# Third mixer's attention by pairs of heads, and heads turned between the chunks of the first two output panels

## What is computed

```python
h = concat(meta, x)                                   # 272 x 1024
for i in range(2):
    h = h + 0.5 * rmsnorm(swiglu(rmsnorm(h)))         # feed-forward, width 2816
    hn = rmsnorm(h)
    m = neighborhood_attention(hn) if i == 0 else diff_attention(hn)
    h = h + rmsnorm(m)
    h = h + 0.5 * rmsnorm(swiglu(rmsnorm(h)))
x = h[16:]                                            # 256 tokens from here on
x = x + rms_norm(hybrid_mixer(rms_norm(x)))           # third mixer
x = x + rms_norm(mlp(rms_norm(x)))                    # width 4096
```

## Time and profile before

| | before |
|---|---|
| median of 3 runs | 1523.96 us (1520.89 to 1527.64) |
| profiled execution, its own time | 1518.83 us |
| its span in the trace | 1517.0 us, granted TensorE clock 0.99 |
| TensorE busy | 1460.0 us (96%) |
| VectorE busy | 955.2 us (63%) |
| ScalarE busy | 659.0 us (43%) |
| GpSimd busy | 53.2 us (4%) |

### The profile page before, as it was taken

One profiled execution on the slowest core, in us unless ns is written; L12 is line 12 of the kernel. 1 busy time (PEld: TensorE's weight loads), 2 busy tenths in 40 slices (PEclk: granted clock), 3 DMA queues, 4 the chain that ended last, 5 costly groups with the idle time before them and its releaser, 6 DMA issues.

```text
span 1517.0 us, 27189 instructions
## 1 busy us (share of the span) xinstructions
PE 1460.0 (96%) x11458; PEld 1404.6 (93%) x11458; DVE 955.2 (63%) x1229; ACT 659.0 (43%) x856; POOL 53.2 (4%) x75
## 2 busy tenths in 40 slices
PE   6999999999999999999999998999999998999998
PEld 5999999978999999999999977899999996999997
DVE  5665567457766646665547566766646657877644
ACT  4444345445544335434335345553434533444432
POOL 0000010011000000000010000100001010100000
PEclk9999999999999999999999999999999999999998
DMA  5555884512455665654464510465555640355551
GB/s 179 171 188 166 224 238 148 175 35 84 140 167 180 177 191 153 195 185 153 149 192 149 170 54 29 141 193 183 173 162 161 197 137 1 112 179 182 193 188 63
DMA packets 250779, 233.52 MB, mean 154 GB/s; under 512 B 29759, under 2 KB 249844, under 8 KB 250688
## 3 DMA queue, kind: packets, MB, share of 16 engines
q1 hardware_dynamic: 250224, 231.96, 49.4%
q10 hardware_dynamic: 464, 0.25, 0.1%
HBM read 230.99 MB, written 1.12 MB: 153 GB/s over the span
## 4 chain that ended last, share of the span: by engine, by line
PE 79%; DVE 10%; issue 4%; ACT 3%; DMA 2%; POOL 1%; SPq 0%; DVEq 0%; ACTq 0%
PE acc L582 23%; PE acc L583 23%; PE acc L584 23%; DVE h L1553 2%; PE aux L747 1%; DVE h L1547 1%; ACT w_hi L1125 1%; DVE rstd L1518 1%; DVE x_lo L1524 1%; PE acc L889 1%; PE acc L919 1%; PE aux L869 1%; PE aux L910 1%; DMA raw<-in_ffn_w_up 1%; DVE h L1608 1%
## 5 line engine op out<-in xcount | busy, mean ns | idle before, releaser
L582 PE MATMUL acc<-x_hi,w_hi 128*128 128x272 f32 (+1 forms) x2096 | 599.2, 286 | 10.5 <-DVE z L1639 6.2
L583 PE MATMUL acc<-x_lo,w_hi 128*128 128x272 f32 (+1 forms) x2096 | 599.9, 286 | 0.0
L584 PE MATMUL acc<-x_hi,w_lo 128*128 128x272 f32 (+1 forms) x2096 | 597.9, 285 | 0.0
L1513 DVE TENSOR_TENSOR w_lo<-raw,w_hi 128x2048 fp32r<-128x2048 f32 (+1 forms) x230 | 483.9, 2113 | 88.5 <-ACT w_hi L1125 88.0
L1125 ACT ACTIVATE w_hi<-raw 128x2048 fp32r<-128x2048 f32 (+3 forms) x251 | 406.6, 1627 | 138.2 <-DMA raw<-in_ffn_w_down 49.6
L582 PEld LDWEIGHTS acc<-x_hi,w_hi 128*128 128x128 f32 x2096 | 396.8, 189 | 12.6 <-issue 10.1
L583 PEld LDWEIGHTS acc<-x_lo,w_hi 128*128 128x128 f32 x2096 | 395.6, 189 | 0.1
L584 PEld LDWEIGHTS acc<-x_hi,w_lo 128*128 128x128 f32 x2096 | 395.6, 189 | 0.0
L582 PE MATMUL acc<-hid_hi,w_hi 128*128 128x272 f32 (+1 forms) x704 | 204.5, 290 | 6.5 <-DVE w_lo L1513 6.5
L583 PE MATMUL acc<-hid_lo,w_hi 128*128 128x272 f32 (+1 forms) x704 | 203.0, 288 | 0.0
L584 PE MATMUL acc<-hid_hi,w_lo 128*128 128x272 f32 (+1 forms) x704 | 201.9, 287 | 0.0
(11 more groups left out here) (295 smaller groups left out, 1621.6 us busy)
## 6 DMA issues: line engine op xcount, KB each, us to landing
raw<-in_ffn_w_gate SPq DMA_DIRECT2D x44, 1024.0 KB, 5.3
raw<-in_ffn_w_up SPq DMA_DIRECT2D x44, 1024.0 KB, 5.3
raw<-in_ffn_w_down SPq DMA_DIRECT2D x32, 768.0 KB, 4.5
raw<-in_ffn_w_down SPq DMA_DIRECT2D x32, 640.0 KB, 4.3
raw<-in_w_up SPq DMA_DIRECT2D x16, 1024.0 KB, 5.3
raw<-in_w_down SPq DMA_DIRECT2D x16, 1024.0 KB, 5.0
raw<-in_na_w_qkv SPq DMA_DIRECT2D x12, 1024.0 KB, 5.2
raw<-in_da_w_qkv SPq DMA_DIRECT2D x12, 1024.0 KB, 5.2
```

The source lines that it names most:

```text
L582: nc.tensor.matmul(o, wh, xh, start=first, stop=False)
L583: nc.tensor.matmul(o, wh, xl, start=False, stop=False)
L584: return nc.tensor.matmul(o, wl, xh, start=False, stop=last)
L1513: nc.vector.tensor_tensor(w_lo[:, slot, w], raw[:, slot, w], w_hi[:, slot, w].bitcast(F32), ALU.subtract)\
```

## The change

Two things are changed.

1. **Pairs in the third mixer.** `attention` and the units of `attention_units` for MIX go; `mix_attention` takes 8 steps, step = (pair m of heads, half t of the queries), on each engine. TensorE's scores of two heads lie on the two halves of the rows. The probabilities get four buffers (`mix_probs`, in x_hi's place), the turned ones two of 512 columns. Keep-warm matmuls stand only in steps 0 and 1. The rotations of the next pair stand at steps 1, 3 and 5. VectorE makes the first two logits ahead of the mLSTM's norm (`inner_norm`), squares at step 5, sums at step 6.
2. **Turns between chunks, behind all three attentions.** `from_heads` turns heads c and multiplies chunk c-2 into panels 0 and 1 together (`shared_chunk`, taken out of `first_panels`). The two panels use all four acc banks, and in the first mixer `turn_heads` now waits for all four evictions before chunk 0 also. Panel 2 goes to aux banks 0 and 1, without a wait for acc; its squares and outputs are read from there, and `sum_rest` waits until they have been read.

With the second go moves of casts and splits. Output panel 1 is cast in step (2,3) of the projection, behind the values, and split there ahead of VectorE's evacuation of that projection panel. Output panel 2 is cast and split behind the eighth chunk's x_hi and x_lo, where output panel 1's were, and no longer at output panel 0. `high` and `low` of panel 3 and of the next phase stand where they stood, SyncE's orders too.

```diff
@@ banks
-            if n % 2 == 0 and n > 0 and isinstance(i, int) and (i, j) == (0, 2):
+            shared = n > 0 if n % 2 == 0 else n // 2 in (NA, DA, MIX)
+            if shared and isinstance(i, int) and (i, j) == (0, 2):
                 return aux[:, 0:2, :]
@@ TensorE
+            def shared_chunk(n, base, tokens, k):
+                    ph = PHASES[n]
+                    pe.wait_ge(x_hi_ready, base + k + 1)
                     for j in range(2):
                         if k == 0:
                             pe.wait_ge(w_lo_ready, ph.p0 + j + 1)
...
-                    pe.wait_ge(x_ready, SPLIT_IN[k_] + k + 1)
+                    pe.wait_ge(x_ready, base + k + 1)
...
-            def from_heads(k_, tokens):
+            def from_heads(k_, tokens, meta):
                 n = 2 * k_ + 1
                 ph = PHASES[n]
-                ready = ready_heads(k_)
-                for j in range(3):
-                    panel(n, 0, j, ph.a0 + j - 1, acc[:, j % 2, :, :], range(8), True, True, x_hi[:, :, 0:tokens],
-                          x_lo[:, :, 0:tokens], ready if j == 0 else lambda k: None)
+                if k_ != NA:
+                    keep_warm(aux[:, 1, :], 10 if k_ == DA else 7)
+                for c in range(8 + 2):
+                    if c < 8:
+                        turn_heads(k_, c, meta)
+                    if c >= 2:
+                        shared_chunk(n, SPLIT_HEADS[k_], tokens, c - 2)
+                panel(n, 0, 2, None, banks(n, 0, 2), range(8), True, True, x_hi[:, :, 0:tokens], x_lo[:, :, 0:tokens],
+                      lambda k: None)
                 last_panel(k_, ph.a0 + 2, range(8), True, x_hi[:, :, 0:tokens], x_lo[:, :, 0:tokens])
...
             def sum_rest(k_, tokens):
+                pe.wait_ge(acc_free, PHASES[2 * k_ + 1].a0 + 3)
                 keep_warm(aux[:, 0, :], 2)
...
+            def mix_attention():
+                s = mixers[MIX]
+                for step in range(8 + 2):
+                    if step in (1, 3, 5):
+                        m = 1 + step // 2
+                        if step == 1:
+                            pe.wait_ge(ml_norm, 4)
+                        rotate_chunk(m, acc_flat[:, 2, :])
+                        rotate_chunk(4 + m, acc_flat[:, 3, :])
+                    if step < 8:
+                        m, t = divmod(step, 2)
+                        w = P * (t + 1)
+                        pe.wait_ge(rope_done, 2 * m + 2)
+                        wait(pe, s["logits"], 2 * step)
+                        if step < 2:
+                            keep_warm(aux[:, 0, 3 * P:], 2)
+                        for b in range(2):
+                            q = slice(64 * b, 64 * b + 64)
+                            nc.tensor.matmul(aux[:, b, 0:w], proj[q, m, P * t:P * t + P], proj[q, 4 + m, 0:w],
+                                             start=True, stop=True).then_inc(s["scores"], 1)
+                    if 1 <= step <= 8:
+                        v = step - 1
+                        nb = v % 2 + 1
+                        pe.wait_ge(s["probs"], 2 * v + 2)
+                        wait(pe, s["turned_copied"], v - 1)
+                        for b in range(2):
+                            for kb in range(nb):
+                                tr = nc.tensor.transpose(aux[:, 2 + v % 2, P * (nb * b + kb):P * (nb * b + kb) + P],
+                                                         mix_probs[:, 2 * (v % 2) + b, P * kb:P * kb + P], ident[:, :])
                         tr.then_inc(s["turned"], 1)
                     if step >= 2:
+                        v = step - 2
+                        m, t = divmod(v, 2)
+                        pe.wait_ge(s["turned_copied"], v + 1)
...
                         mm.then_inc(s["pv"], 1)
@@ turn_heads
-                    if k == NA and c % 4 == 0:
-                        pe.wait_ge(s["evicted"], 2 + c // 2)
+                if k == NA and c % 4 == 0:
+                    pe.wait_ge(s["evicted"], 4)
@@ ScalarE
-                    if local <= last - 2:
+                    if local <= last - 2 and (groups_of > 1 or local > 0):
                         high(n, i, j + 2)
...
-                        if (i, j) != (2, 3) and (i, j) not in ((0, 0), (0, 1)):
+                        if (i, j) not in ((0, 0), (0, 1)):
                             high(n, i, j + 2)
...
-                        high(n, 2, 5)
+                    high(n + 1, 0, 2)
@@ VectorE
+            def mix_attention(inner_norm, between):
+                s = mixers[MIX]
+                for step in range(8 + 1):
+                    if step < 8:
+                        m, t = divmod(step, 2)
+                        w = P * (t + 1)
+                        for b in range(2):
+                            u, col = 2 * step + b, 4 * m + 2 * b + t
+                            dve.wait_ge(s["scores"], u + 1)
+                            wait(dve, s["probs"], u - 1)
...
+                    if step == 0:
+                        inner_norm()
+                    if step in (1, 3, 5):
+                        m = 1 + step // 2
+                        rope_chunk(m, acc_flat[:, 2, :])
+                        rope_chunk(4 + m, acc_flat[:, 3, :])
+                    if step >= 1:
+                        v = step - 1
+                        w = 2 * P * (v % 2 + 1)
                         dve.wait_ge(s["turned"], v + 1)
                         wait(dve, s["pv"], v - 1)
+                        nc.vector.tensor_copy(turned_pair[:, v % 2, 0:w], aux[:, 2 + v % 2, 0:w])\
                             .then_inc(s["turned_copied"], 1)
+                    between(step)
...
+                        if (i, j) == (2, 3):
+                            split(n, i, j)
                         evacuate(n, i, j, tokens, dst, p, SCALE if queries else None)
...
-                    low(n, 2, 5)
+                    low(n + 1, 0, 2)
```

233 lines of the change are left out of this document (69 added, 164 removed).

## The result

The changed kernel took 1542.63 us (median of 4 runs, 1540.99 to 1543.82), the kernel before 1522.43 in runs beside them: ratio 1.0137, 95% interval 1.0115 to 1.0159, 20 us slower. Forecast was 1529.8, with a range up to 1538.0: the sign of "somewhat slower" was right, the size wrong by 13 us. The profiled execution's span went from 1517.0 to 1542.0 us, its mean granted clock from 0.99 to 0.975. These spans lie 25.0 us apart and the medians 20.2, because the profiled execution of the kernel before took 3.6 us less than its median and that of the changed kernel 1.2 us more.

A forecast was written before the change was run, and what follows sets the result against it. TensorE, with 79% of the chain, was taken as the bound. First mixer +4.5, second -0.05, third +0.45 and clock +0.9 made +5.8 us: 1524.6 profiled, 1529.8 as median; range 1518 to 1538.

The forecast's parts named there:

- 1. When T comes: Interleaved turns and panels behind each attention shift output panel 1's end: +1.65 us first mixer, -2.9 second, -1.55 third.
- T: The moment output panel 1 is done behind an attention; in the first mixer 368.07 us before, 369.7 forecast.
- 2. What T releases: At each output, next-phase loads go as a pair, the second landing later: +2.85 us at each of three outputs.
- 3. The weight splits: Moved splits: +1.15 us at the third mixer's entry; some 2.5 us w_lo wait before each last panel, hidden by squares.
- The cover: Slack at each ones-matmul, TensorE arriving before the squares' sum: 0.95 us in the first mixer, 1.55 in the others.
- 4. The clock: Half-clock falls behind TensorE's new waits at the outputs, mostly hidden: +0.9 us, 0 to 5 if not hidden.
- Rival A: Each output's two new or longer waits bring the half clock onto the path: +14.8 us, 1538.8; chance 0.24.
- 5. The pairs: Third mixer's attention by pairs takes 27.75 us instead of 29.75: -2.0 us; at full clock 26.15, -3.6.
- B: Third mixer's pairs run at VectorE's pace, 10.2 us gained instead of 2.0: -2.4 us, 1521.6; chance 0.10.
- C: At the outputs the doubled transfer is hidden and TensorE's own arrival counts: +1.75 us, 1525.7; chance 0.06.
- D: Faster by over 0.5%, B and C together: -6.45 us, 1517.5, or -8.1 with first mixer's late turns free; chance 0.08.

The follow-up runs named there:

- turns_only: The changed kernel with the third mixer's attention by units again, turns, casts, splits and panels still changed; 1535.59 us, ratio 1.0093.
- unscale_late: The changed kernel, but at the three outputs VectorE splits the last output panel ahead of unscaling h; 1544.80 us, ratio 1.0166.
- pairs_only: The kernel before with only the third mixer's attention by pairs; turns, casts, splits and panels as before; 1524.66 us, ratio 1.0019.
- pairs_warm: The kernel before with the third attention by pairs and keep-warm matmuls fitted to its waits, 2 instead of 1 per mLSTM step; 1521.28 us, ratio 1.0006.
- split_quarters: The changed kernel, third mixer's output panel 1 split in quarters in VectorE's mLSTM gaps, not ahead of the last evacuation; 1535.07 us, ratio 1.0090.
- before_delayed: The kernel before with 82 more keep-warm matmuls ahead of panel (1,0) of the third mixer's projection; 1546.24 us, ratio 1.0160.
- mended_units: The changed kernel with quartered split and cast, unscaling in pieces, earlier squares, table load and turns, fitted keep-warm matmuls, third attention by units; 1515.26 us, ratio 0.9982.
- warm_entry: The changed kernel with 18 instead of 8 keep-warm matmuls ahead of TensorE's wait for the third mixer's last projection panel; 1541.33 us, ratio 1.0135.

## Why the prediction was wrong, by its steps

**1. When T comes.** Second mixer: forecast -2.9, measured -2.5 (T at about 955.05, where the stage came 9.0 later). Right. First mixer: forecast +1.65, measured +3.5 (T at 371.1). The wait and the two turns were priced, the half clock behind the wait of 1.80 us was not: 1.5 us in this execution, nothing in five others, which leaves +2.0. Third: forecast -1.55, measured -0.2, because it began at half clock (1298 to 1306); in turns_only, at full clock there, T came 15.2 us behind the eviction, for 15.15 forecast.

**2. What T releases.** The pair of loads was right: issues 0.58 us apart, the second landing after 7.86 us (7.6 forecast), 2.9 us behind the first. By its own terms the landing should have stood at T + 8.05, not T + 8.15; it came at T + 8.4. From T to the ones-matmul the working gave 14.55; in the changed kernel it is 16.2, 15.2 and 15.4. In the first mixer the chain of squares had 0.26 us more in the transfer and 1.4 more in GpSimd's sum (4.10 for 2.72), which no term had. In unscale_late, with TensorE's other wait out of the way, it is 15.6, with GpSimd's two sums at 4.4 us together.

**3. The weight splits.** The +1.15 at the third mixer's entry is exact (a wait of 1.16 us), and what it costs is not: +1.15 was written down for a move that cost 7.6 us by itself. The w_lo wait before the last panel came as forecast (3.38, 2.31 and 2.06 us against "some 2.5"), a little longer in the first mixer: VectorE's reciprocal, unscaling and outputs took 7.5 us there, not 6.4. VectorE's rows of the changed kernel, then GpSimd's:

```profile
371.01 1.84 DVE L1567 RECIPROCAL rstd<-sd 128x272 f32<-128x272 f32 x1
372.88 3.80 DVE L1574 TENSOR_TENSOR h<-h,rstd 128x544 f32<-128x544 f32 x4
376.61 1.96 DVE L1505 TENSOR_SCALAR y<-acc,gains 128x272 f32<-128x272 f32 x4
380.69 4.48 DVE L1479 TENSOR_TENSOR w_lo<-raw,w_hi 128x2048 fp32r<-128x2048 f32 x2
```

```profile
374.15 1.95 POOL L2187 TENSOR_TENSOR sq_sum<-sq_sum,sq 128x544 f32<-128x544 f32 x1 [27.05 <-ACT sq L1117]
382.31 4.09 POOL L2187 TENSOR_TENSOR sq_sum<-sq_sum,sq 128x544 f32<-128x544 f32 x1 [6.21 <-ACT sq L1117]
```

In the kernel before, the same four unscalings with GpSimd idle, and GpSimd's two sums of this size at the first output:

```profile
525.92 2.63 DVE L1608 TENSOR_TENSOR h<-h,rstd 128x544 f32<-128x544 f32 x4
369.17 1.37 POOL L2215 TENSOR_TENSOR sq_sum<-sq_sum,sq 128x544 f32<-128x544 f32 x1 [21.61 <-ACT sq L1142]
376.15 2.71 POOL L2215 TENSOR_TENSOR sq_sum<-sq_sum,sq 128x544 f32<-128x544 f32 x1 [5.61 <-ACT sq L1142]
```

The four unscalings took 3.80 us beside a sum of GpSimd and 2.63 without one. GpSimd's last sum took 4.09 us beside two splits, which kept their 2.2 to 2.3 each; it ended 1.3 us behind the second split, about what one sum takes alone (1.37), as if it had stood behind both. The Trainium skill, "Advanced Engine Details and Errata", section "VectorE Performance Modes", says that VectorE's second port is shared with GpSimd and that GpSimd's instructions and VectorE's two-port instructions block each other. Its table gives a tensor_tensor no two-port mode, yet by these rows tensor_tensor and GpSimd's sum hold each other up.

The last panel then started at half clock (0.57 from 381 to 385). So TensorE came to the ones-matmul at T + 16.0, not T + 13.6, and waited only 0.17 us more for the squares' sum. The cover that the working counted on was used up, and the two queues ended together.

**4. The clock.** This is the step that failed: "+0.9". The working priced falls only where the change makes new waits at the outputs, and only behind waits over 2 us, since that was what the earlier trace rows showed. A wait of 1.16 us ahead of a thin stretch was enough. Rival A, "the clock decides", had a chance of 0.24 and the price of 14.8 us. Its direction came true, its places mostly did not: of its six waits two were followed by the half clock, those ahead of the last panel in the first and second mixer, and TensorE still had to wait 0.17 and 0.32 us for the squares' sum behind them. What the half clock cost in the changed kernel's trace lies elsewhere: 5.4 us in the mLSTM part; some 4.4 in the attention, of which 1.6 stood in step 5; 1.5 in the first mixer's first chunks; and 1.3 in the third mixer's T, by turns_only. That is 11.0 us beyond what steps 1 to 3 and 5 held, against 0.9.

The rest of the 19.2 us between the spans' 25.0 and the forecast's 5.8 is 3.1 from T to the ones-matmuls (step 2), 2.9 in the two long stretches, and smaller differences, the largest 2.4 in the attention, whose cause stays open.

The Trainium skill, "TensorE: Matmul & The Clock Gate", section "HAM oscillation — how this bites in real kernels", tells of waits for a transfer, each of which leaves the next work cold. Here it was not each: the waits of 2.06 and 1.80 us at the third output were not followed by the half clock, and the one of 1.80 us at the first output was in five of ten profiles.

**5. The pairs.** Forecast 27.75 with a fall behind the inner norm, measured 32.92 (32.45 alone). By the rope's milestones in pairs_only: 10.3 us to the first new rope (9.55 forecast), 8.0 to the next (5.35), 5.5 to the third (5.35), 8.65 for the last pair (7.5). (The kernel before had 6.15 and 6.6 for the second and third, where the working says 6.6 for both.) The second is the half clock, which did not end behind the rotations but went on over the whole first pair, with waits for the rope in it (4.2 us in three in the changed kernel). At full clock the working had 26.15 and pairs_warm took 28.03, so that about half of the forecast gain of 3.6 us was there; 25.78 came only with the squares and their sum moved out of the last pair. The half clock that pairs_warm leaves to the stage behind, some 1.2 us, was in no term. The change had also taken out the keep-warm matmuls between the units, which I had read in the diff and not priced.

Rivals B, C and D did not occur.

**What stays open.** Why split_quarters and before_delayed fell in the mLSTM part without a wait, and why the single runs of one kernel, the kernel before too (1518.5 to 1532.2), fall into groups by their clock. The rows show the clock and what TensorE did ahead of it, and these were alike in profiles that fell and profiles that didn't, at the first output's 1.80 us too. Open as well is how much of the changed kernel's 20 us comes back in the clock alone: no run kept it at 1.00 at the outputs and changed nothing else.

## What to carry to other kernels

A wait of TensorE is priced by what it works on next: 1.17 us ahead of a stretch with two thirds of a panel's matmul records cost 7.6 us, while 2.06 us ahead of a full panel cost no clock in seven of nine profiles. One profile is one draw: before a half clock is put down to a wait, look whether kernels with the same wait have it too. Take keep-warm matmuls out of a chain of waits only with their clock in the sum, and size them to the wait.

Here two queues ended within 2 us of each other, and mending one showed nothing clear of the noise; mend both before such a reorder is judged. The kernel with the interleaving and the pairs was 20 us slower than before, and 4.0 to 7.5 us faster once the work behind the panels had been moved into the idle time that the interleaving opens on VectorE and ScalarE, and its waits filled.

## What was not expected of the hardware

The clock stayed at 0.50 through the mLSTM part while TensorE counted as busy for all of the window (8.00 of 8.00 us from 1258): work without a gap in the records did not bring it back there. The same kernel kept or lost the clock from run to run, for 6 to 8 us of difference (before_delayed, mended_units). At one place, the first output's wait of 1.80 us, ten profiles with the same instructions up to there split into five at half clock and five not. And a keep-warm call is dearer than I read it: each is two records, 0.23 us in all. The 18 of warm_entry:

```profile
1247.71 4.18 PE L748 MATMUL aux<-ones 128*128 128x128 f32 x36
```
